# A weight's high part ahead of an evacuation, and the first round of a channel mixer in another order

## The reference, cut to what matters

```python
px = split_proj(modulate(x, pre_mix_g[l], mx[0], mx[1]) @ w_in[l])
...
x = x + mx[2] * rms_norm(mix_x, post_mix_g[l])
hx = swiglu(modulate(x, pre_ffn_g[l], mx[3], mx[4]), ffn_w_gate[l], ffn_w_up[l], ffn_w_down[l])
x = x + mx[5] * rms_norm(hx, post_ffn_g[l])
```

## Time and profile before

| | us |
|---|---|
| median of 3 runs | 1495.44 |
| lowest and highest | 1494.52, 1496.35 |
| the profiled execution | 1495.62 |
| its span, first to last instruction | 1493.8 |

### The profile page before, as it was taken

The page is one execution under the profiler, slowest core; times in us unless marked ns, Lnnn a source line. Parts: engine busy times, 40 slices in busy tenths (PEclk is TensorE's granted clock), DMA queues, the critical chain, the costliest instruction groups (busy, mean ns, idle before and its releaser), DMA issues. The chain is left out here.

```text
span 1493.8 us, 17710 instructions
## 1 busy us (share of the span) xinstructions
PE 1392.7 (93%) x6773; PEld 1161.9 (78%) x6773; DVE 787.5 (53%) x1050; ACT 367.1 (25%) x530; POOL 325.9 (22%) x135
## 2 busy tenths in 40 slices
PE   6698999899899998897978999999999999999998
PEld 2587888788788877686756788888888888888876
DVE  2999878669768876818831223231322323132227
ACT  3511222232232133615422111112121111112112
POOL 1521111111121024503423212212212221221110
PEclk9699899999999997999989999999999999999999
DMA  9393011010010010004311101110110111011032
GB/s 366 144 314 122 29 31 41 1 56 14 28 42 28 14 68 31 1 18 152 113 43 57 57 29 57 57 55 30 56 56 28 56 56 55 29 56 56 30 140 113
DMA packets 94703, 101.93 MB, mean 68 GB/s; under 512 B 3118, under 2 KB 77091, under 8 KB 94658
## 3 DMA queue, kind: packets, MB, share of 16 engines
q1 hardware_dynamic: 94658, 101.32, 19.9%
HBM read 92.92 MB, written 8.39 MB: 68 GB/s over the span
## 5 line engine op out<-in xcount | busy, mean ns | idle before, releaser
L1227 POOL TENSOR_TENSOR slot<-slotraw,slot 128x1024 fp32r<-128x1024 f32 x66 | 158.7, 2426 | 533.3 <-ACT slot L1163 342.4
L560 PE MATMUL bank<-h2Ta,slot 128*128 128x512 f32 x1056 | 248.7, 395 | 14.2 <-POOL slot L1227 11.7
L560 PE MATMUL bank<-slot,mid 128*128 128x512 f32 x1056 | 244.7, 393 | 5.4 <-DVEq L1715 3.6
L560 PEld LDWEIGHTS bank<-h2Ta,slot 128*128 128x128 f32 x1056 | 201.1, 191 | 57.4 <-POOL slot L1227 12.4
L560 PEld LDWEIGHTS bank<-slot,mid 128*128 128x128 f32 x1056 | 200.4, 190 | 48.2 <-DVEq L1715 4.0
L560 PE MATMUL bank<-cathi,slot 128*128 128x512 f32 x704 | 221.8, 392 | 5.9 <-POOL catlo L1227 5.9
L560 PE MATMUL bank<-hT,ringb 128*128 128x512 f32 (+1 forms) x672 | 157.1, 392 | 14.1 <-POOL ringb L1227 14.1
L1410 DVE SCALAR_TENSOR_TENSOR cat<-conv_u,taps,cat 128x784 f32 (+29 forms) x120 | 155.7, 1298 | 12.6 <-DVE cat L1410 6.2
L560 PEld LDWEIGHTS bank<-cathi,slot 128*128 128x128 f32 x704 | 133.1, 189 | 33.9 <-issue 6.1
L560 PEld LDWEIGHTS bank<-hT,ringb 128*128 128x128 f32 x672 | 124.6, 198 | 38.4 <-issue 10.1
L1679 DVE TENSOR_TENSOR mid<-bank,sgm 128x512 f32<-128x512 f32 x44 | 30.4, 692 | 233.7 <-ACT sgm L1178 233.7
(11 more groups left out here) (168 smaller groups left out, 1517.5 us busy)
## 6 DMA issues: line engine op xcount, KB each, us to landing
mraw<-in_w_mod SPq DMA_DIRECT2D x48, 512.0 KB, 7.0
slotraw<-in_ffn_w_gate SPq DMA_DIRECT2D x22, 512.0 KB, 3.7
slotraw<-in_ffn_w_up SPq DMA_DIRECT2D x22, 512.0 KB, 4.8
slotraw<-in_ffn_w_down SPq DMA_DIRECT2D x22, 512.0 KB, 3.9
ringinb<-in_w_in SPq DMA_DIRECT2D x12, 512.0 KB, 3.7
xst<-in_x SPq DMA_DIRECT2D x8, 512.0 KB, 13.8
ringina<-in_w_in SPq DMA_DIRECT2D x8, 512.0 KB, 4.7
ringinc<-in_w_in SPq DMA_DIRECT2D x8, 512.0 KB, 4.7
```

The lines of the kernel that those rows point to most:

```text
L560: return pe.matmul(o, l, r, start=start, stop=stop, skip_group_check=True)
L1227: return pool.tensor_tensor(lo, full, hi.bitcast(F32), ALU.subtract)
```

## The change

It has these edits.

- ScalarE makes the value weight's high part before the evacuation of unit 13, not behind it.
- The h2 pieces are shared: VectorE evacuates the four of bank 6, ScalarE the four of bank 7. `h2_free` now counts VectorE's share once per tile and a new semaphore `h2_used` ScalarE's. ScalarE's `gu_hi(0, 2)` and `gu_hi(0, 3)` stand at the beginning of tiles 4 and 6, not at the end.
- POOL makes the low parts of the first four weights behind the h2 low parts of tiles 0, 1, 3 and 5.
- `turn2(7)` stands directly behind `turn2(6)`.
- SP loads slot 3 in its step 5, and refills each slot when that slot's last product is done, not in pairs or all together.
- In round 1 VectorE copies the gate row between its two pairs.

```diff
@@ sync @@
                 if t == 4:
                     load_ffn(2, 0, GU[2])
-                if t == 6:
+                if t == 5:
+                    sp.wait_ge(mix_done, 5)
                     load_ffn(3, 0, GU[3])
...
                     for j in range(4):
-                        if j % 2 == 0:
-                            sp.wait_ge(gu_full, n * 8 + (8 if first(n) else 2 * j + 4))
+                        sp.wait_ge(gu_full, n * 8 + (j + 5 if first(n) else 4 * (j // 2) + 3 + j % 2))
                         load_ffn(j, n + 1, GU[j])
@@ tensor @@
                     if t >= 1:
-                        pe.wait_ge(h2_free, 2 * t - 1 + half)
+                        pe.wait_ge(h2_used if half else h2_free, t)
...
                         gate_up(n, pos, j)
-                        if first(n) and pos < 2:
+                        if first(n) and 2 * pos + j < 3:
                             turn2(4 + 2 * pos + j)
+                            if 2 * pos + j == 2:
+                                turn2(XT - 1)
@@ scalar @@
+                    if u == last_unit(NTILE - 2):
+                        head_hi(s, NTILE - 1)
                     evac(s, u)
...
-                    if u == last_unit(NTILE - 2):
-                        head_hi(s, NTILE - 1)
...
             def h2_part(t):
-                act.wait_ge(h2_free, 2 * t + 2)
+                act.wait_ge(h2_full, 2 * t + 2)
+                if t:
+                    act.wait_ge(h2_lo, t)
+                for k in range(4, KT):
+                    step(act.activation(h2f[:, k, :], bank[7][:, (k - 4) * P:(k - 3) * P], ACT.Identity,
+                                        scale=gain2[:, k:k + 1], bias=mod[:, 3, k, 0:1]))
+                step.wait()
+                act.sem_inc(h2_used, 1)
+                act.wait_ge(h2_free, t + 1)
                 act.activation(h2_block(t, 0), h2f[:], ACT.Copy).then_inc(h2_hi, 1)
...
             for t in range(XT + 1):
+                if t == 4 or t == 6:
+                    gu_hi(0, t // 2)
                 if t < XT:
                     x1_root_(t)
...
-                if t == 4 or t == 6:
-                    gu_hi(0, t // 2)
@@ gpsimd @@
-            for j in range(2):
-                ffn_lo(j, j)
             for t in range(XT):
-                if t == 4 or t == 6:
-                    ffn_lo(t // 2, t // 2)
                 pool.wait_ge(h2_hi, t + 1)
                 lo_part(h2_block(t, 1), h2f[:], h2_block(t, 0)).then_inc(h2_lo, 1)
+                if t in (0, 1, 3, 5):
+                    ffn_lo((t + 1) // 2, (t + 1) // 2)
@@ vector @@
-                for k in range(KT):
-                    if k % 4 == 0:
-                        dve.wait_ge(h2_full, 2 * t + k // 4 + 1)
-                    if k == 0 and t:
-                        dve.wait_ge(h2_lo, t)
+                dve.wait_ge(h2_full, 2 * t + 1)
+                if t:
+                    dve.wait_ge(h2_lo, t)
+                for k in range(4):
...
             def dve_round(n, par):
                 dve_pair(n, 0, par)
-                dve_pair(n, 1, par)
                 if isinstance(n, int) and n == 1:
                     dve.wait_ge(g_full, 1)
...
+                dve_pair(n, 1, par)
```

More of the change, by code:

```diff
@@ L334, in kernel_program @@
         mix_full, mix_root, mix_done, x1_root = sem("mix_full"), sem("mix_root"), sem("mix_done"), sem("x1_root")
+        h2_used = sem("h2_used")
         x2_ready, h2_full, h2_free, h2_hi, h2_lo = (sem("x2_ready"), sem("h2_full"), sem("h2_free"),
@@ L884, in pe_round @@
                         gate_up(n, pos, j)
-                        if first(n) and pos < 2:
+                        if first(n) and 2 * pos + j < 3:
                             turn2(4 + 2 * pos + j)
+                            if 2 * pos + j == 2:
+                                turn2(XT - 1)
                     if isinstance(n, int) and n == 1 and pos == 1:
-                        pe.wait_ge(h2_free, 2 * XT)
+                        pe.wait_ge(h2_free, XT)
+                        pe.wait_ge(h2_used, XT)
                         gate_rows()
@@ L1647, in h2 @@
             def h2(t):
-                for k in range(KT):
-                    if k % 4 == 0:
-                        dve.wait_ge(h2_full, 2 * t + k // 4 + 1)
-                    if k == 0 and t:
-                        dve.wait_ge(h2_lo, t)
-                    ins = dve.tensor_scalar(h2f[:, k, :], bank[6 + k // 4][:, (k % 4) * P:(k % 4 + 1) * P],
+                dve.wait_ge(h2_full, 2 * t + 1)
+                if t:
+                    dve.wait_ge(h2_lo, t)
+                for k in range(4):
+                    ins = dve.tensor_scalar(h2f[:, k, :], bank[6][:, k * P:(k + 1) * P],
                                             gain2[:, k:k + 1], mod[:, 3, k, 0:1], ALU.mult, ALU.add)
-                    if k % 4 == 3:
-                        ins.then_inc(h2_free, 1)
+                ins.then_inc(h2_free, 1)
             mix_add(0)
```

## The result

The changed kernel takes 1458.62 us (median of 4 runs, 1457.22 to 1461.15) against 1495.12 for the kernel before on the same chip: ratio 0.9751, 95% interval 0.9739 to 0.9764, so 36.5 us less. The forecast was 1454.3 us, in a range of 1447 to 1466. The profiled execution took 1457.22 us with a span of 1455.3; against the profiled execution before that is 38.4 us less, where the forecast's sum was 41.3.

The account below looks back on a forecast made before the run. TensorE, busy 93% of the span, was taken as the bound, so time could come only from its holes and low clock. Terms 0.7 + 16.0 + 24.6 = 41.3 us off 1495.62 gave 1454.3 us, range 1447 to 1466.

Parts of the forecast that it names:

- part 1: Value weight's high part made earlier in the heads: 0.7 us in head 0 plus 16.0 in heads 1 to 3.
- part 2: Channel mixer's entry and first rounds: holes of TensorE close or shrink, 19.4 + 5.2 = 24.6 us.
- rival C: Head 0 keeps its whole gain because the taps' end does not count: 1448.8 us; chance 0.05.
- The tail: Stretch after head 3: its work shifts with the heads' gain; a rival had 5.4 us absorbed there, 1459.7 us, chance 0.13.
- (a): Channel mixer's entry, tile 0: without POOL's weight parts before h2, x2 is ready 2.2 us earlier.
- Rival B: POOL's moved weight parts block VectorE in four tiles, everything behind 4.4 us late: 1458.7 us; chance 0.12.
- (b): h2 tiles: VectorE evacuates four pieces, not eight; its period falls from 8.16 to 6.9 us, first gate product at 723.4.
- (c): Before the fourth product: its 4.50 us hole and slow block go; a new 2.5 us hole stands before transposes 7.
- (d): Second half waits for tile 7's low part, 752.9 against 767.96: 15.1 us, plus 2.1 for the clock; 1.4 hole left.
- (e): Before round 1: reloading slots one by one removes ScalarE's 2.23 us load wait; 5.0 of the 7.23 us hole stay.
- (f): First down product: earlier gate row copies remove the 3.57 us wait and 1.6 us of slow stretch, together 5.2 us.
- Rival D: h2 hand-overs between engines serialise and set the tile period; with 14 us it gives 1504.7 us; chance 0.02.

Follow-up runs that it names:

- head0_rows: Changed kernel with VectorE's last four modulation rows made before head 0's last four taps, not behind them: 1453.57 us, ratio 0.9720.
- loads_old: Changed kernel with the old waits for reloading slots 0 to 3 (all four after round 0, then in pairs): 1457.80 us, ratio 0.9749.
- pool_old: Changed kernel with POOL making the first two weights' low parts ahead of the loop over tiles again: 1458.85 us, ratio 0.9746.
- gate_old: Changed kernel with VectorE's gate row copies behind both pairs of round 1 again: 1464.49 us, ratio 0.9784.

## Why the prediction was right, and where it was off

The mechanism was right in most parts: the holes named closed or shrank for the reasons given, and the trace's sum is off by 2.8 us, mostly in three terms. By the medians 36.5 us came where 41.1 were forecast (1495.44 less 1454.3): part 1 gave 13.4 to 14.5 of 16.7, part 2, taken as the rest, 21.9 to 23.0 of 24.6.

- **Part 1.** Heads 1 to 3 gave 16.4 us against 16.0: hole and slow block both went. Head 0 gave 0.4 against 0.7 in the profiled execution and nothing in the seven others that can be compared. The forecast moved the hole onto VectorE's row, and `head0_rows` shows that the taps were the cover, so rival C is out. It left out that POOL's parts move too: one of them made the taps 2.0 us longer and the gate row 1.7 shorter, so that its 0.7 came near by luck.
- **The tail was taken at nothing**, on the ground that each engine there is released by TensorE or by the head's end. The waits did shift with it. What the step left out is the clock: 1.3 us in the profiled execution. This is the largest mis-sized term. By the medians part 1 lost 2.3 to 3.4 us (16.8 less 14.5 or 13.4), of which the runs do not tell how much is the tail's and how much head 0's.
- **(a)** came as forecast in place and size, 2.2 us in the profiled execution. Undone alone it is worth 1.9 us in traces with the same clock and nothing that the medians can tell. Rival B's mechanism, POOL's parts under VectorE's two-input operations, is at work in tiles 1 and 2, but that it gives back all that tile 0 gained is not shown. The rule of the Trainium skill, SBUF — State Buffer, on the shared port pair, fits the rows looked at: the blocked operation of 1024 elements ended 1.07 us after POOL's part in the kernel before (686.76) and 1.08 after it in the changed kernel (684.15 and 689.21).
- **(b)** 2.4 against 3.2. Four ScalarE pieces took 1.48 to 1.51 us (estimate 1.6). VectorE's pieces of tile 0 and of tile 3 are 23.3 us apart (679.31 and 702.58), 2.6 more than three periods of 6.9, where I had put 1.8 for the meetings: the missing 0.8.
- **(c), (d)** 9.4 against 9.7. The hole before transposes 7 is 2.57 us (2.5). The hole of 1.4 before the second half did not come, because a fall of the clock that I had not forecast (transposes 1.97, product 6.45 us) lay over it. Two errors that cancel.
- **(e)** 4.89 us of hole were left against 5.0, but `loads_old` shows the 2.2 us as 1.3 to 2.4 in the traces and as nothing in the medians. The step priced a shortened hole without the slow stretch behind it.
- **(f)** 4.5 against 5.2: the wait is gone; the slow stretch behind the hole before round 1 is 1.0 us longer than before (13.92 against 12.96); it is 0.7 us or more longer in five of the seven traces with that hole. "None before the first down product" held; the wait of 1.8 us on a slot that the table shows stands before the last block and was there before.

Rival D is out: TensorE's periods in tiles 1 and 2 stayed at 7.7 us. The weight of the edits, each undone alone, was not where the sum put it: shared pieces 7.3 us, transposes 7 in their new place 6.9, the gate row 4.9, the low parts and the reloads nothing that the medians tell. The sum went by position in one trace, where edits that close one hole together can't be told apart.

## What to carry to other kernels

Price a hole of TensorE together with the slow stretch behind it, and take that stretch from more than one trace: shortening one by 2.4 us, from 7.3 to 4.9, was worth 1.3 to 2.4 us in the traces, and all but closing it gave 6.9 us. Before counting on a removed wait, look for the row that ends next to it on another engine; in head 0 a move of four small rows in VectorE's program was worth 3.7 us in the trace and 5.0 by the medians, of about 6 that were hidden. Ask also which other parts move when a weight comes earlier, and what they will meet. When several edits serve one stretch, undo each alone: two of five were worth nothing that the medians could tell. And compare two traces only where their clocks agree: 1.3 of the 3.1 us of `pool_old` were the clock's.

## What the hardware showed that I had not expected

- **The clock also falls behind short waits.** Behind 2.57 us of waiting (before transposes 7) the granted clock is 0.56, and in the tail it is 0.60 from 611 to 615, behind waits of 1.40, 1.54 and 0.74 us with few matmuls between them. The changed kernel, windows of its timeline before transposes 7 and behind the hole before round 1:

```profile
730.00:732.00 2.00, 1.56 (x8) 1.56 (x9) 0.39 (x1) 0.58 (x1) 1.34 (x1) 0.56 0.38 154
765.00:769.00 4.00, 3.69 (x9) 2.91 (x10) 0.00 (x0) 2.56 (x3) 4.00 (x3) 0.50 0.00 0
```

- **The same instructions give other slow stretches.** From the last recurrence product to the first mix product the eleven traces with part 1 take 64.65 to 68.45 us (eight of them 65.5 or more), the two without it 64.7 and 64.9. In the changed kernel the clock is low behind the waits on `catlo`; in `gate_old` it is at 1.00 in and behind those waits (608 to 620) and low over the first mix products (0.55 and 0.60 from 664 to 672), and the transposes of tile 0 then come 10.05 us after the first mix product instead of 8.79. Whether the 3.9 us by which runs of the changed kernel differ come from there was not tried.
- **POOL is slowed too.** A low part of 128 x 1024 takes 2.35 to 2.4 us alone and up to 3.34 to 3.39 beside VectorE's work, and VectorE's 1.28 us update takes 3.23 where POOL's part began first.
